# Gated recurrence in chunks of 64 tokens, two chunks side by side in the output partitions, in place of chunks of 128

## The chip, the cores and the metric

The kernel runs on one core of one Trainium2 chip. The time is device microseconds of one execution; the median of three runs is compared. The engines are TensorE (PE in the rows, with its weight loads as PEld), VectorE (DVE), ScalarE (ACT), GpSimd (POOL) and the DMA queues that SyncE (SP) and the others issue.

## What is computed

One inference step of one layer: a combined projection of 512 prompt tokens and 64 decode tokens (8 sequences of 8), a sparse attention with an indexer, a gated recurrence (HGRN2), an output projection and a layer norm. The change touches the recurrence alone. It has 4 heads with a 128x128 state each; the reference writes it chunk by chunk:

```python
cum = jnp.cumsum(gc, axis=2)
o_inter = jnp.einsum('bhtk,bhkv->bhtv', qc * jnp.exp(cum), S)
rel = jnp.where(causal, cum[:, :, :, None, :] - cum[:, :, None, :, :], -jnp.inf)
scores = jnp.einsum('bhtk,bhsk,bhtsk->bhts', qc, kc, jnp.exp(rel))
o_intra = jnp.einsum('bhts,bhsv->bhtv', scores, vc)
last = cum[:, :, -1:, :]
S_new = (jnp.exp(last[:, :, 0, :])[..., None] * S
         + jnp.einsum('bhsk,bhsv->bhkv', kc * jnp.exp(last - cum), vc))
```

The size of the chunk changes only the rounding of the result, not what is computed.

## The kernel before

**Layout.** Everything is float32. `qa`, `ky`, `cum`, `dec`, `kE` and `qE` lie with the 128 key dimensions in the partitions and 576 tokens (512 of the prompt, 64 of decode) by 4 heads in the free dimension. `ia` (the values), `sc` (the scores within a chunk) and `kdT` lie with tokens in the partitions.

**Scores within a chunk, by levels.** `exp(rel)` depends on both tokens and on the key dimension, so the kernel splits the causal triangle into levels. Level 0 is the diagonal. Level l > 0 has a block size b of 1, 2, 4, up to 64: a query in the right half of a block of 2b tokens meets a key in the left half, and both are scaled relative to the cumulative gate at the edge between the halves. For each level VectorE makes the right half of the differences into `dec` (L1389), GpSimd the left half (L1581), ScalarE takes the exponential of all of `dec` (L1114), GpSimd makes `kE` (L1591) and VectorE `qE` (L1460). TensorE multiplies `kE` by `qE` for a tile of 128 tokens and 4 heads: this is one job of a level (`level_job`, L808), and the levels with b below 8 have a fifth job for the decode tokens. VectorE copies the part that belongs to the level out of PSUM by a mask (`scores_out`, L1401) into `sc`.

**What they are interleaved with.** The same loops run the prompt attention: 32 pairs of a head and a block of 128 queries, pair a with block b = a % 4. A step is: logits (L821), masked row maximum on VectorE (L1409), exponential on ScalarE (L1092), transpose on TensorE (L830), copy of the transposed on ScalarE (`probs_out`, L1100), times values on TensorE (L839), scaled output on VectorE (L1421). The order is written out by hand: level l has three steps, from `LEAD + STEP * l` on, with `LEAD, STEP = 2, 3`. Three jobs stand in its first step and the others in its second. In the first step VectorE also makes the differences of level l + 1; ScalarE takes their exponential at the head of the second step, after `probs_out` of the first; VectorE makes `qE` in the third. The decay of the queries and of the keys to the end of the chunk follows at step `LAST`, `LAST + 1` and `LAST + 2`, where `LAST = LEAD + STEP * NLEV` is 26. The steps 29 to 31 and the two that drain have attention alone; the whole from step 26 on is called the tail here.

**The recurrence** stands in a second block, after all of this. TensorE turns `kE` into `kdT`, then for each of 4 chunks c makes the chunk's share of the state (L1694, into PSUM bank 4 + c % 2), turns a tile of the attention's output (`turn_gated`, L1680), and makes the output from the scores within the chunk (L1702) and from the state before it (L1706). VectorE makes the new state (`new_state`, L1899), copies the outputs (`outputs`, L1905) and then normalizes and gates (`norm_and_gate`, L1928). VectorE's order is `new_state(c)`, `outputs(c - 1)`, `mean_square(c - 2)`, `norm_and_gate(c - 3)`. GpSimd spreads decode values over `vx` (L1869), the last two when the outputs are done. TensorE goes on with `turn_normed(0)` (L1724), which waits for `norm_and_gate(0)`, then with the decode outputs (L1742, L1745) and the output projection (L1776) to the end.

## Time and profile before

| | |
|---|---|
| median of 3 runs | 785.72 us (784.81 to 791.41) |
| profiled execution, its own time | 787.79 us |
| its span, first to last instruction | 786.1 us |
| TensorE busy / weight loads | 734.3 us (93%) / 433.9 us |
| VectorE, ScalarE, GpSimd busy | 491.0, 265.0, 238.1 us |
| mean granted TensorE clock | 0.968 |
| levels with attention | 569 to 649 us |
| the tail | 649 to 676 us |
| recurrence, up to `turn_normed(0)` | 676 to 697 us |

A clock of 1.00 is 2.4 GHz and 0.50 is 1.2 GHz. A float32 matmul stands in the trace as two records of MATMUL and two of LDWEIGHTS, a transpose as one of each; so 12 matmuls are x24. Busy times are of one profiled execution.

### The profile page before, as it was taken

How to read it: one execution, taken by the hardware profiler on the slowest of the kernel's cores; microseconds unless marked ns; L12 is line 12 of the kernel's file. 1: busy time of each engine (PE TensorE's matmuls, PEld its weight loads, DVE VectorE, ACT ScalarE, POOL GpSimd, SP SyncE). 2: the span in 40 equal slices, each digit the busy share in tenths (PEclk: the TensorE clock that was granted, in tenths of full speed). 3: DMA queues.
4: the chain of work that ended last, by engine and by line, in shares of the span. 5: the costliest groups of instructions: out<-in, count | busy, mean ns of one | idle time of the engine just before them, and what ended most of it. 6: DMA issues, size and time to landing. Idle time of an engine off the chain costs nothing. (4 is left out here: it accounts for less than half of the span.)

```text
span 786.1 us, 13385 instructions
## 1 busy us (share of the span) xinstructions
PE 734.3 (93%) x4554; PEld 433.9 (55%) x4554; DVE 491.0 (62%) x923; ACT 265.0 (34%) x571; POOL 238.1 (30%) x342
## 2 busy tenths in 40 slices
PE   4688999999999899999999999999999997989994
PEld 3344444544444455767655566774477774864441
DVE  0213399999999546545555645555489985294535
ACT  3104710235665122223223222226556444340000
POOL 2610013046987223222222222221143461450000
PEclk9899999999999899999999999999999996699998
DMA  9900063060400588988888899861040000510611
GB/s 229 376 17 1 4 212 115 1 220 1 167 1 0 161 252 257 348 262 282 290 253 256 257 306 310 279 191 43 14 200 2 1 1 0 159 70 0 199 55 41
DMA packets 61316, 114.68 MB, mean 146 GB/s; under 512 B 8370, under 2 KB 21763, under 8 KB 61251
## 3 DMA queue, kind: packets, MB, share of 16 engines
q1 hardware_dynamic: 31122, 52.28, 21.7%
q0 software_dynamic: 12448, 40.27, 15.1%
q10 hardware_dynamic: 17680, 21.30, 8.1%
q8 instruction: 37, 0.61, 0.3%
q14 instruction: 29, 0.23, 0.1%
HBM read 106.60 MB, written 7.23 MB: 145 GB/s over the span
## 5 line engine op out<-in xcount | busy, mean ns | idle before, releaser
L473 PE MATMUL banks<-wbuf,xT 128*128 128x512 f32 (+1 forms) x448 | 147.4, 533 | 5.5 <-DMA wbuf<-in_w_in 5.5
L338 POOL DMA_DIRECT2D arena<-in_cache_v x128 | 70.0, 547 | 205.3 <-issue 205.3
L473 PEld LDWEIGHTS banks<-wbuf,xT 128*128 128x128 f32 (+1 forms) x448 | 65.8, 176 | 81.1 <-issue 70.8
L733 PE MATMUL banks<-wbuf,xT 128*128 128x512 f32 (+1 forms) x288 | 101.2, 531 | 0.0
L1262 DVE TENSOR_REDUCE small<-banks 128x1 f32<-128x512 f32 x32 | 22.1, 692 | 98.6 <-PE banks L664 98.6
L1220 DVE MAX8 small<-arena 64x8 f32<-64x2112 f32 x32 | 75.1, 2348 | 1.3
L1222 DVE MATCH_REPLACE8 arena<-small,arena 64x2112 f32<-64x2112 f32 x32 | 74.7, 2334 | 0.0
L647 PE MATMUL banks<-ident,arena 128*128 128x128 f32 x512 | 69.0, 278 | 4.1 <-DVE wbuf L1255 3.8
L647 PEld LDWEIGHTS banks<-ident,arena 128*128 128x128 f32 x512 | 57.1, 142 | 25.7 <-issue 19.3
L719 PE MATMUL banks<-xT,arena 128*128 128x288 f32 x256 | 67.4, 406 | 0.0
L1028 ACT COPY wbuf<-banks 128x512 f32<-128x512 f32 x64 | 37.2, 582 | 75.8 <-PE banks L647 69.8
L733 PEld LDWEIGHTS banks<-wbuf,xT 128*128 128x128 f32 (+1 forms) x288 | 41.0, 174 | 35.7 <-issue 32.8
L1035 ACT ACTIVATE arena<-banks,small 128x512 f32<-128x512 f32 x32 | 22.0, 688 | 96.5 <-DVE small L1262 96.5
L719 PEld LDWEIGHTS banks<-xT,arena 128*128 128x128 f32 x256 | 46.1, 190 | 10.1
L1503 POOL TENSOR_TENSOR arena<-arena,rope 128x64 f32<-128x64 f32 (+4 forms) x60 | 19.2, 350 | 93.8 <-ACT arena L890 92.4
L1537 POOL TENSOR_TENSOR late<-late,arena 128x256 f32<-128x256 f32 (+2 forms) x45 | 44.9, 999 | 6.0 <-ACT arena L964 0.8
L1255 DVE COPY wbuf<-banks 128x512 f32<-128x512 f32 x64 | 43.4, 679 | 0.8 <-PE banks L647 0.8
L808 PE MATMUL banks<-arena 128*128 128x128 f32 (+1 forms) x288 | 35.1, 275 | 6.1 <-DVE arena L1460 3.2
L808 PEld LDWEIGHTS banks<-arena 128*128 128x128 f32 (+1 forms) x288 | 31.9, 185 | 13.9 <-issue 9.7
L1275 DVE COPY arena<-banks 128x512 f32<-128x512 f32 x32 | 22.1, 689 | 27.3 <-PE banks L684 27.3
L695 PEld LDWEIGHTS banks<-arena 128*16 128x16 f32 x1024 | 25.1, 96 | 17.5 <-issue 17.5
L695 PE MATMUL banks<-arena 128*16 128x128 f32 x1024 | 34.1, 274 | 0.0
(256 smaller groups left out, 1139.7 us busy)
## 6 DMA issues: line engine op xcount, KB each, us to landing
arena<-in_cache_k SPq DMA_DIRECT2D x128, 256.0 KB, 3.4
arena<-in_cache_v POOLq DMA_DIRECT2D x128, 256.0 KB, 3.8
wbuf<-in_w_in ACTq DMA_DIRECT2D x8, 2048.0 KB, 12.8
arena<-in_w_in ACTq DMA_DIRECT2D x8, 512.0 KB, 6.0
arena<-in_x_prompt SPq DMA_DIRECT2D x8, 256.0 KB, 6.0
wbuf<-in_w_out SPq DMA_DIRECT2D x1, 2048.0 KB, 9.0
xT<-in_w_out SPq DMA_DIRECT2D x1, 2048.0 KB, 13.7
arena<-in_x_prompt SPq DMA_DIRECT2D x4, 512.0 KB, 8.4
```

The source lines that it names most:

```text
L338: e.dma_start(buf[n % 2][:, i, :], cache[bass.ds(pg, 1), 0].rearrange("a p h d -> p (a h d)")).then_inc(arrived[n % 2], 16)
L473: mm = pe.matmul(psum[a * NS:a * NS + ROWS[t], n % PB, 0:w // split], xT[:, c, t * P:t * P + ROWS[t]], wbuf[:, WB[g], c, a * w // split:(a ...
L647: mm = pe.transpose(psum[:, KB0 + j % 2, i * P:(i + 1) * P], k_buf[n % 2][:, i, j * P:(j + 1) * P], ident[:])
L695: mm = pe.matmul(psum[32 * j:32 * j + 16, OB, g * P:(g + 1) * P], pT[n % 2][:, i * P + 32 * j:i * P + 32 * j + 16], v_buf[n % 2][:, i, j * ...
L719: mm = pe.matmul(psum[:, FB, 0:HALF], w_f[m % 2][:, c, :], xT[:, c, half * HALF:(half + 1) * HALF], start=(c == 0), stop=(c == KC - 1), sk ...
L733: mm = pe.matmul(psum[a * NS:a * NS + ROWS[t], bank, 0:512 // split], xT[:, c, t * P:t * P + ROWS[t]], wbuf[:, WB[g], c, a * 512 // split: ...
L808: mm = pe.matmul(psum[0:w, n % 3, h * w:(h + 1) * w], kk[:, h, c0:c0 + w], qq[:, h, c0:c0 + w], start=True, stop=True, skip_group_check=True)
L1028: nc.scalar.copy(kg[n % 2][:, j, :], psum[:, KB0 + 1, :]).then_inc(kg_act, 1)
L1220: nc.vector.max(best[0:NS, 0, :], S).then_inc(topk, 1)
L1222: nc.vector.match_replace(S, best[0:NS, 0, :], S, TAKEN).then_inc(topk, 1)
L1255: nc.vector.tensor_copy(kg[n % 2][:, j, :], psum[:, KB0, :]).then_inc(kg_dve, 1)
L1537: nc.gpsimd.tensor_tensor(SP[b], SP[b], src, ALU.add).then_inc(pacc, 1)
```

## The change

A chunk is 64 tokens (`CH`), so the prompt has 8 chunks (`NC`) and the level with b = 64 is gone; `NLEV` is 7 and `LAST` is 23. Two chunks that follow each other still share a tile of 128 tokens: in a level job the first chunk's 64x64 scores go to partitions 0 to 63 and the second's to 64 to 127, by two matmuls for each head in place of one, and the mask and `sc` are half as wide. In the recurrence each step makes the shares of two states (keys and values from one half of the partitions each), the outputs within two chunks, then the outputs from the state before, for one chunk after the other, each in half of the output partitions. There are 8 state updates, and the outputs are copied from two banks, by halves of the partitions. The outputs of the second chunk now take banks 6 and 7 too, so `turn_normed(0)` and the decode outputs wait for the last of those copies (`oc_ev`). Two buffers that decode had shared with the masks have places of their own.

```diff
-LEVELS = [0, 1, 2, 4, 8, 16, 32, 64]
+LEVELS = [0, 1, 2, 4, 8, 16, 32]
+CH = 64
+NC = SEQ // CH
...
-        sc = carve(NT * 512).rearrange("p (c n) -> p c n", c=NT)
+        sc = carve(NT * HA * CH).rearrange("p (c n) -> p c n", c=NT)
...
-                    w, c0 = (P, c * P) if c < NT else (NS, SEQ)
                     for h in range(HA):
-                        mm = pe.matmul(psum[0:w, n % 3, h * w:(h + 1) * w], kk[:, h, c0:c0 + w], qq[:, h, c0:c0 + w],
-                                       start=True, stop=True, skip_group_check=True)
+                        for a in range(2 if c < NT else 1):
+                            c0 = c * P + a * CH
+                            mm = pe.matmul(psum[a * CH:(a + 1) * CH, n % 3, h * CH:(h + 1) * CH], kk[:, h, c0:c0 + CH],
+                                           qq[:, h, c0:c0 + CH], start=True, stop=True, skip_group_check=True)
                     mm.then_inc(lv, 1)
...
-                        out, mask, src = sc[:, c], levels[:, l], psum[:, n % 3, :]
+                        out, mask, src = sc[:, c], levels[:, l], psum[:, n % 3, 0:HA * CH]
...
-                for c in range(NT):
-                    pe.wait_ge(turned_ev, c + 1)
-                    if c >= 2:
-                        pe.wait_ge(st_ok, HA * (c - 1))
+                def chunk_states(t):
+
+                    pe.wait_ge(turned_ev, t + 1)
+                    if t:
+                        pe.wait_ge(st_ok, HA * 2 * t)
                     for h in range(HA):
-                        mm = pe.matmul(psum[:, 4 + c % 2, h * P:(h + 1) * P], kdT[:, c, h * P:(h + 1) * P],
-                                       ia[:, c, h * P:(h + 1) * P], start=True, stop=True, skip_group_check=True)
+                        for a in range(2):
+                            r = slice(a * CH, (a + 1) * CH)
+                            mm = pe.matmul(psum[:, 4 + a, h * P:(h + 1) * P], kdT[r, t, h * P:(h + 1) * P],
+                                           ia[r, t, h * P:(h + 1) * P], start=True, stop=True, skip_group_check=True)
                     mm.then_inc(kv, 1)
-                    turn_gated(c)
-                    if c >= 2:
-                        pe.wait_ge(oc_ev, c - 1)
+
+                def chunk_out(t, a):
+                    r = slice(a * CH, (a + 1) * CH)
+                    return r, psum[r, (2, 6)[a] + t % 2, :]
+
+                def within_chunks(t):
+                    if t >= 2:
+                        pe.wait_ge(oc_ev, t - 1)
                     for h in range(HA):
-                        out = psum[:, 2 + c % 2, h * P:(h + 1) * P]
-                        mm = pe.matmul(out, sc[:, c, h * P:(h + 1) * P], ia[:, c, h * P:(h + 1) * P],
-                                       start=True, stop=(c == 0), skip_group_check=True)
-                        if c:
-                            pe.wait_ge(st_ok, HA * c)
-                            mm = pe.matmul(out, qE[:, h, c * P:(c + 1) * P], states[(c - 1) % 2][:, h * P:(h + 1) * P],
-                                           start=False, stop=True, skip_group_check=True)
-                    mm.then_inc(oc, 1)
+                        for a in range(2):
+                            r, out = chunk_out(t, a)
+                            mm = pe.matmul(out[:, h * P:(h + 1) * P], sc[r, t, h * CH:(h + 1) * CH],
+                                           ia[r, t, h * P:(h + 1) * P], start=(h == 0), stop=(t == 0 and a == 0),
+                                           skip_group_check=True)
+
+                def from_before(t):
+                    for a in range(2):
+                        cc = 2 * t + a
+                        if cc == 0:
+                            continue
+                        pe.wait_ge(st_ok, HA * cc)
+                        r, out = chunk_out(t, a)
+                        for h in range(HA):
+                            mm = pe.matmul(out[:, h * P:(h + 1) * P], qE[:, h, cc * CH:(cc + 1) * CH],
+                                           states[(cc - 1) % 2][:, h * P:(h + 1) * P], start=False, stop=True,
+                                           skip_group_check=True)
+                        mm.then_inc(oc, 1)
+
+                for t in range(NT):
+                    chunk_states(t)
+                    turn_gated(t)
+                    within_chunks(t)
+                    from_before(t)
...
                     pe.wait_ge(mixed, t + 1)
+                    if t == 0:
+                        pe.wait_ge(oc_ev, NT)
...
                 values_apart(1)
-                pool.wait_ge(oc, NT)
+                pool.wait_ge(oc, NC - 1)
...
-                    dve.wait_ge(kv, c + 1)
+                    dve.wait_ge(kv, c // 2 + 1)
                     if c >= 2:
-                        dve.wait_ge(oc, c)
+                        dve.wait_ge(oc, c - 1)
...
-                        dve.wait_ge(oc, t + 1)
-                        nc.vector.tensor_copy(oa[:, t, :], psum[:, 2 + t % 2, :]).then_inc(oc_ev, 1)
+                        for a in range(2):
+                            r = slice(a * CH, (a + 1) * CH)
+                            dve.wait_ge(oc, 2 * t + a if t else 1)
+                            ins = nc.vector.tensor_copy(oa[r, t, :], psum[r, (2, 6)[a] + t % 2, :])
+                            if a == 0:
+                                me.add(ins)
+                        me.wait()
+                        ins.then_inc(oc_ev, 1)
...
                 for c in range(NT):
-                    new_state(c)
+                    new_state(2 * c)
+                    new_state(2 * c + 1)
                     if c >= 1:
                         outputs(c - 1)
```

TensorE in a middle level, before: logits (L821), three jobs (L808), a transpose and values of other steps (L830, L839), and in the second step the fourth job and the decode job.

```order
L821 MATMUL banks<-late 128x256
L808 MATMUL banks<-arena 128x128 x12
L830 MATMUL banks<-ident,wbuf 128x128
L839 MATMUL banks<-v_tok,wbuf 128x128 x4
L821 MATMUL banks<-late 128x384
L808 MATMUL banks<-arena 128x128 x4
L808 MATMUL banks<-arena 64x64 x4
L830 MATMUL banks<-ident,wbuf 128x128 x2
```

The same place after (line numbers are 4 higher):

```order
L825 MATMUL banks<-late 128x256
L812 MATMUL banks<-arena 64x64 x24
L834 MATMUL banks<-ident,wbuf 128x128
L843 MATMUL banks<-v_tok,wbuf 128x128 x4
L825 MATMUL banks<-late 128x384
L812 MATMUL banks<-arena 64x64 x12
L834 MATMUL banks<-ident,wbuf 128x128 x2
```

Nothing moved; 12 matmuls of 128 columns have become 24 of 64. The fourth job's 8 and the decode job's 4 are now one row of 12.

TensorE in the recurrence, the third chunk before: share of the state, `turn_gated`, and then for each head the two matmuls of the output.

```order
L1694 MATMUL banks<-arena 128x128 x4
L1680 MATMUL banks<-ident,late 128x128 x4
L1702 MATMUL banks<-arena 128x128
L1706 MATMUL banks<-arena 128x128
L1702 MATMUL banks<-arena 128x128
L1706 MATMUL banks<-arena 128x128
L1702 MATMUL banks<-arena 128x128
L1706 MATMUL banks<-arena 128x128
L1702 MATMUL banks<-arena 128x128
L1706 MATMUL banks<-arena 128x128
```

After, one pair of chunks (L1700 `chunk_states`, L1714 `within_chunks`, L1726 `from_before`):

```order
L1700 MATMUL banks<-arena 128x128 x8
L1683 MATMUL banks<-ident,late 128x128 x4
L1714 MATMUL banks<-arena 64x128 x8
L1726 MATMUL banks<-arena 64x128 x8
```

There are 24 matmuls where 12 stood, and all of those that read a state stand last.

VectorE at the end of the recurrence before: the last `new_state`, `outputs(2)`, `mean_square(1)`, `norm_and_gate(0)` (its reciprocal and four products), `outputs(3)`.

```order
L1899 SCALAR_TENSOR_TENSOR arena<-arena,banks 128x128 x4
L1905 COPY arena<-banks 128x512
L1919 TENSOR_SCALAR small<-small 128x4
L1925 RECIPROCAL small<-small 128x4
L1928 SCALAR_TENSOR_TENSOR arena<-arena,small 128x128 x4
L1905 COPY arena<-banks 128x512
```

The same place after:

```order
L1928 SCALAR_TENSOR_TENSOR arena<-arena,banks 128x128 x8
L1936 COPY arena<-banks 64x512 x2
L1954 TENSOR_SCALAR small<-small 128x4
L1960 RECIPROCAL small<-small 128x4
L1963 SCALAR_TENSOR_TENSOR arena<-arena,small 128x128 x4
L1936 COPY arena<-banks 64x512 x2
```

Two state updates and two half copies stand where one of each stood.

## Rows read from the trace of the kernel before

**Rows 1.** Stretches: us, busy us of PE, PEld, DVE, ACT, POOL, then PEclk, DMA.
```profile
615.00:625.00 10.00, 8.94 (x62) 7.05 (x61) 9.89 (x19) 4.92 (x10) 4.27 (x2) 1.00 0.01 2
...
652.00:654.50 2.50, 0.39 (x4) 0.18 (x3) 2.46 (x6) 0.04 (x1) 0.00 (x0) 0.92 0.00 0
...
661.00:676.20 15.20, 12.96 (x43) 8.98 (x42) 4.39 (x19) 3.48 (x10) 1.94 (x2) 0.50 0.00 1
676.20:681.40 5.20, 5.20 (x24) 4.51 (x25) 0.00 (x0) 2.90 (x5) 5.20 (x5) 0.50 0.67 189
...
692.60:697.00 4.40, 1.84 (x15) 1.25 (x14) 4.40 (x5) 1.37 (x10) 3.91 (x2) 1.00 0.20 60
697.00:701.90 4.90, 4.90 (x48) 3.90 (x50) 4.67 (x19) 2.06 (x11) 0.79 (x1) 0.65 0.02 3
```

**Rows 2.** Timeline of one middle level: start, us, engine, line.
```profile
621.73 2.75 PEld L808 LDWEIGHTS banks<-arena 128*128 128x128 f32 x24 [1.12 <-issue]
...
621.81 1.90 POOL L1581 TENSOR_TENSOR arena<-arena 128x1024 f32<-128x1024 f32 x1 [1.23 <-DVE arena L1460]
621.97 2.81 DVE L1389 TENSOR_TENSOR arena<-arena 128x1024 f32<-128x1024 f32 x1
...
625.05 1.95 DVE L1401 COPY_PREDICATED arena<-arena,banks 128x512 f32<-128x512 uint8 x3
...
625.67 0.24 ACT L1100 COPY wbuf<-banks 128x128 f32<-128x128 f32 x1
625.81 1.91 ACT L1114 ACTIVATE arena<-arena 128x2048 f32<-128x2048 f32 x1
...
627.80 2.35 POOL L1591 TENSOR_TENSOR arena<-arena 128x1024 f32<-128x1024 f32 x1 [4.10 <-ACT arena L1114]
...
629.76 1.47 DVE L1460 TENSOR_TENSOR arena<-arena 128x1024 f32<-128x1024 f32 x1
...
631.30 2.75 PEld L808 LDWEIGHTS banks<-arena 128*128 128x128 f32 x24 [1.05 <-issue]
```

**Rows 3.** Timeline: ahead of the exponential of the first level.
```profile
571.78 0.38 PE L830 MATMUL banks<-ident,wbuf 128*128 128x128 f32 x2
...
572.19 0.37 ACT L1100 COPY wbuf<-banks 128x256 f32<-128x256 f32 x1 [1.27 <-PE banks L830]
...
572.46 2.13 ACT L1114 ACTIVATE arena<-arena 128x2304 f32<-128x2304 f32 x1
```

**Rows 4.** Timeline: outputs of two attention steps in the tail.
```profile
664.33 0.28 DVE L1421 SCALAR_TENSOR_TENSOR late<-banks,small,late 128x64 f32<-128x64 f32 x1 [1.88 <-PE banks L839]
...
675.58 0.28 DVE L1421 SCALAR_TENSOR_TENSOR late<-banks,small,late 128x64 f32<-128x64 f32 x1 [2.23 <-PE banks L839]
```

**Rows 5.** Groups of one shape, 540 us to the end.
```profile
L1401 DVE COPY_PREDICATED arena<-arena,banks 64x256 f32<-64x256 uint8 x4 | 1.7, 425 | 0.0
...
L1990 DVE SCALAR_TENSOR_TENSOR arena<-arena,banks 64x512 f32<-64x512 f32 x1 | 0.7, 679 | 2.6 <-PE banks L1784 2.6
```

**Rows 6.** Timeline: weight loads of a 64-column job.
```profile
574.45 0.54 PEld L808 LDWEIGHTS banks<-arena 128*64 128x64 f32 x8
```

**Rows 7.** The chain that ended last: start, us, what.
```profile
686.49 0.89 PE banks L1694 x8
...
689.60 0.91 PE banks L1694 x8
...
690.53 1.12 DVE arena L1899 x4
...
692.45 4.43 DVE arena L1928 x4
...
696.92 0.66 PE banks L1724 x4
...
701.65 2.02 PE banks L1745 x32
```

**Rows 8.** Timeline of POOL in the recurrence.
```profile
692.80 3.91 POOL L1869 TENSOR_TENSOR arena<-arena,ofseq 64x1024 f32<-64x1024 f32 x2 [7.97 <-PE banks L1706]
```

More of the change, by code:

```diff
@@ L81, in shape_constants @@
     c["gather"] = np.concatenate([16 * (p // 16 == np.arange(8)[None, :]), p % 16], 1).astype(np.float32)
-    c["levels"] = lv.reshape(P, len(LEVELS) * P)
+    c["levels"] = lv.reshape(P, len(LEVELS) * CH)
     keep = np.ones((P, TOK), np.float32)
-    keep[:, 0:SEQ:P] = 0
+    keep[:, 0:SEQ:CH] = 0
     keep[:, SEQ::NNEW] = 0
@@ L351, in hybrid_step @@
         dec, cum, qE = (carve(4 * TOK).rearrange("p (h n) -> p h n", h=HA) for _ in range(3))
-        sc = carve(NT * 512).rearrange("p (c n) -> p c n", c=NT)
+        sc = carve(NT * HA * CH).rearrange("p (c n) -> p c n", c=NT)
         sc_n = carve(HA * NS)[0:NS]
-        levels_mem = carve(len(LEVELS) * HA * P // 4)
+        levels_mem = carve(len(LEVELS) * HA * CH // 4)
         levels = levels_mem.bitcast(U8).rearrange("p (l n) -> p l n", l=len(LEVELS))
-        levels_f = spare[:, 3072:3072 + len(LEVELS) * P].rearrange("p (l n) -> p l n", l=len(LEVELS))
+        levels_f = spare[:, 3072:3072 + len(LEVELS) * CH].rearrange("p (l n) -> p l n", l=len(LEVELS))
         states = [carve(HA * P) for _ in range(2)]
         seqcols = carve(NSEQ * NS)
+        apart_v, apart_q = carve(NSEQ * P), [carve(NSEQ * NS) for _ in range(2)]
         xflat = xT[:].rearrange("p c n -> p (c n)")
@@ L1370, in masks_in @@
                     for h in range(HA):
-                        me.add(nc.vector.tensor_copy(levels[:, :, h * P:(h + 1) * P], levels_f))
+                        me.add(nc.vector.tensor_copy(levels[:, :, h * CH:(h + 1) * CH], levels_f))
                     me.wait()
@@ L1436, in to_chunk_end @@
                     dve.wait_ge(qc_ok, 1)
-                    for (a, b, w) in ((0, SEQ, P), (SEQ, TOK, NNEW)):
+                    for (a, b, w) in ((0, SEQ, CH), (SEQ, TOK, NNEW)):
                         v = cum[:, :, a:b].rearrange("p h (n r) -> p h n r", r=w)
@@ L1619, in hybrid_step @@
         vx = [v[0:NS, a * 1024:(a + 1) * 1024].rearrange("p (s n) -> p s n", s=NSEQ)
-              for v in (vflat, scflat) for a in range(2)]
-        qx = [v.rearrange("p (s n) -> p s n", s=NSEQ) for v in (bias_p[:, 0:512], bias_p[:, 512:1024],
-                                                                levels_mem[:, 0:512], levels_mem[:, 512:1024])]
+              for v in (vflat, scflat, apart_v) for a in range(2) if a < v.shape[1] // 1024][0:HA]
+        qx = [v.rearrange("p (s n) -> p s n", s=NSEQ) for v in (bias_p[:, 0:512], bias_p[:, 512:1024], *apart_q)]
         sq = vflat[:, 2048:2048 + W2]
@@ L1653, in _ @@
                 sp.dma_start(lnb, ln_b.partition_broadcast(P)).then_inc(ln_in, 16)
-                sp.wait_ge(st_ok, HA * NT)
+                sp.wait_ge(st_ok, HA * NC)
                 sp.dma_start(st_prompt[0, 0].rearrange("h k v -> k h v"),
-                             states[(NT - 1) % 2].rearrange("p (h n) -> p h n", h=HA)).then_inc(state_st, 16)
+                             states[(NC - 1) % 2].rearrange("p (h n) -> p h n", h=HA)).then_inc(state_st, 16)
                 sp.wait_ge(skv_ev, HA)
@@ L1898, in new_state @@
                                 dve.wait_ge(st_ok, HA * c)
-                            nc.vector.scalar_tensor_tensor(st, old, el_p[:, h * NT + c:h * NT + c + 1], src,
+                            nc.vector.scalar_tensor_tensor(st, old, el_p[:, h * NC + c:h * NC + c + 1], src,
                                                            ALU.mult, ALU.add).then_inc(st_ok, 1)
```

13 lines of the change are left out of this document (7 added, 6 removed).

## The prediction

> **What bounds the kernel now.** I read the stretches first, then the timeline of one middle level, then the chain that ended last. The three places that the change touches have three different limits.
>
> In the levels (569 to 649 us) the limit is a ring through three engines, and the jobs of TensorE and the masked copies are not in it. Follow one level in [rows 2]. VectorE's `qE` product ends at 621.7 and TensorE's jobs begin. GpSimd makes its differences until 623.7, VectorE its own until 624.8. VectorE then has a row maximum, ScalarE an exponential of the attention and the copy `probs_out` at 625.67, and only then comes the exponential of the level, 625.81 to 627.72. GpSimd's product runs 627.80 to 630.15 and VectorE's `qE` product ends at 631.23, 1.1 us behind it. The next jobs begin at 631.30. The level took 9.57 us. The three jobs took 2.75 us and end at 624.5, ahead of the differences; the three masked copies took 1.95 us and end at 627.0, when VectorE's next product can't yet begin. The `qE` product shows the same: it was started at 629.76, ahead of the end of GpSimd's product, and still ended 1.1 us behind that end. So VectorE is busy nearly always here (9.89 of 10 us from 615 to 625, [rows 1]) and yet not the limit: what it gains in the copies it will spend waiting.
>
> In the tail TensorE runs at 1.2 GHz ([rows 1]: PEclk 0.50 from 661 on; it fell behind 652 to 654.5, where TensorE was busy 0.39 us of 2.50). It is busy 12.96 of 15.20 us, and four attention steps take 675.58 - 664.33 = 11.25 us [rows 4], 2.81 us each.
>
> In the recurrence the chain runs through TensorE and, at the end, VectorE [rows 7]: chunk 2 begins at 686.49, chunk 3 at 689.60, so 3.11 us a chunk; then the last state (1.12, from 690.53), a copy and two small operations (0.8 together), `norm_and_gate(0)` (4.43, from 692.45), and TensorE resumes at 696.92. From there TensorE is the limit to the end, so what resumes later ends later.
>
> **Prices of the new matmuls.** Eight records of 128 columns take 0.89 us (L1694, [rows 7]): 0.111 each. Eight weight loads of 64 columns with 64 moving columns take 0.54 us [rows 6], at most 0.068 a record. Do two halves of the output partitions run side by side? L1745 does what the change does: matmuls of 64 weight columns, alternating between the halves, 128 moving columns. Its 32 records took 2.02 us [rows 7], 0.063 each, where one after the other would need 0.111. They overlap. TensorE: Matmul & The Clock Gate, in the Trainium skill, says under Part 3 that weight loads overlap running matmuls only when the row groups differ. L1745's pairs share their row group, so this trace disagrees; by that rule the first and last level below would lose 1 us rather than gain 2.2, and the sum would be 3.2 us higher.
>
> A group of three jobs, 24 records and 2.75 us before, is 48 records: 48 x 0.068 / 2 = 1.6 us if the pairs overlap, 3.2 us if they do not. I take 1.6, since L1745 is the nearest row. In the middle levels either is hidden behind the differences (3.1 us after the jobs begin), so their jobs cost and save nothing. Without that cover, 3.2 us would cost 0.5 a level.
>
> **The masked copies.** A copy of 256 columns takes 0.425 us (64 partitions, [rows 5]) against 1.95 / 3 = 0.65: 28 copies save 6 us of VectorE. By the ring above I count zero; if VectorE were the limit it would be all 6.
>
> **The level that goes.** It takes 9.57 us with it. But the 32 attention steps stay, and three of them ran under it. They now run bare in the tail: 3 x 2.81 = 8.4. Gain 1.1 us. `LAST` comes three steps earlier and its work is the same. At 2.4 GHz the bare steps would be cheaper, so 8.4 is the upper end.
>
> **First and last level.** In the first the exponential (572.46) waited for `probs_out`, and that for the transposes at 571.78, which stand behind three jobs [rows 3]. With 1.6 for 2.75 all moves up 1.1 us. The last level has no differences under it, and its four jobs are in the path of the attention: 32 records at 0.111 are 3.6, 64 at 0.034 are 2.2. Of these 1.4 I take 1.1, since ScalarE has its own waits. Together -2.2, between +1 (no overlap) and -2.5.
>
> **The recurrence, ring.** Each pair of chunks now needs: shares of two states 16 x 0.063 = 1.0; `turn_gated` 4 x 0.111 = 0.44; within the chunks 16 x 0.063 = 1.0; the first chunk's output from its state 8 x 0.111 = 0.89. Only then may VectorE overwrite the older buffer with the second state (1.12), and the next pair's shares wait for that, since both their banks must be read. The second chunk's output (0.89) runs beside it. With 0.5 for draining, semaphores and changes of tile shape (my estimate, from the gaps of 0.02 to 0.1 us between engines in [rows 2]) it is 4.95 against 3.11. The first pair has no state to wait for at its start: +1.3. The next two: +1.84 each. So the fourth pair begins 5.0 us later.
>
> **The recurrence, end.** Before, from the start of chunk 3 to TensorE's resuming: 696.92 - 689.60 = 7.3. After, from the start of pair 3: 1.0 + 0.44 + 1.0 + 0.89 + 0.5 = 3.8; state 7, 1.12; `outputs(2)` is two copies, and a copy of 64 partitions costs the same as one of 128 (0.679 for 64x512, [rows 5]), so 1.3; two small operations 0.3 at most (0.8 less a copy). `norm_and_gate(0)` took 4.43 because it ran beside two GpSimd products of 3.91 us [rows 8]; those now begin about 1.7 us ahead of it, so it should end at about 9.2. TensorE must also wait for `outputs(3)`, 1.3 more, which stands behind it in VectorE's queue: before it was in nobody's way. That is 10.4, +3.1. Queued behind this new wait on TensorE are `turn_normed(0)`, the decode outputs and the projection. Both parts: +8.1 us.
>
> **The clock.** From 697 to 701.9 it was 0.65 [rows 1]: low for 3.4 us of 4.9, behind a wait of TensorE, which was busy 1.84 of the 4.40 us ahead of it. That wait grows from 2.5 to about 5 us, so I expect the low stretch to cover more of the decode outputs: +0.8, between 0 and 2. The head of the recurrence ran at 0.50 until 681.4 [rows 1]; the rise may come a little later with thinner work: +0.4, between 0 and 2.
>
> **Sum.** -1.1 - 2.2 + 5.0 + 3.1 + 1.2 = +6.0 us. The profiled execution took 787.79 us (span 786.1), so such a one would take 793.8; against the median of 785.72 it is **791.7 us**, 0.8% slower. About 1% (7.9 us) is what a measurement of this kernel can tell from no change.
>
> **Rivals.**
> - *The row halves do not run side by side (slower).* The shares of two states take their keys from partitions 0 to 63 and 64 to 127; no pair in this trace has different rows, so L1745 does not vouch for them. Then each of the eight groups costs 16 x 0.111 = 1.8, 0.8 more, all in the ring: +6.2, 798 us. It decides at a price of 0.078 a record, where the total passes 7.9. 15%.
> - *The clock (slower).* The levels keep TensorE less busy with jobs, and the recurrence has more waits. If it falls to 1.2 GHz in some levels, TensorE's work there becomes the limit for a while; if it does not rise in the recurrence, pieces of 3.3 us a pair double. 3 to 14 us more, 795 to 805; I put 798. For it: one short gap was enough at 652. Against: the levels had gaps of a microsecond ahead of each group of jobs [rows 2], and ran at 1.00 [rows 1]. 14%.
> - *VectorE is the limit in the levels after all.* -6 us: 786. Against it stands the `qE` product in [rows 2]. 9%.
> - *The clock stays up in the tail.* The gap at 652 falls otherwise, eight or more steps cost some 1.9 in place of 2.8 us (my estimate: TensorE's part halves, the other engines' part stays): -7, 785. 10%.
> - *The change does not do what it says:* the order shows the matmuls halved in width and doubled in number, and seven levels; under 1%.
>
> **How the numbers follow.** The forecast, 789 to 795, has 51%. A quarter of it lies past +1%; of the two slower rivals nearly all. The two that come out near the old time are within 1%, together a little below it in one case of four. So: slower 0.40, same 0.53, faster 0.07. The range has to hold both the clock's rivals and the row halves' price: 784 to 800 us.
>
> **What the profile after would show.** Middle levels still 9.6 us from jobs to jobs, VectorE with new idle time ahead of `qE`, masked copies near 0.4 us. Three jobs in about 1.6 us. Four bare steps in the tail still 11.2 us at 0.50. In the recurrence 4.9 us from pair to pair, `turn_normed(0)` released by `outputs(3)` some 29 us after the block's start in place of 20.7. I am wrong if the levels shrink with the copies, if the pairs of 16 records take 1.8 us, or if the clock behaves otherwise.

## The result and the profile after

The changed kernel takes 789.88 us (median of 20 runs, 786.34 to 794.28) beside 787.08 us for the kernel before (20 runs). The ratio is 1.0037, with a 95% interval of 1.0019 to 1.0054: 2.9 us slower, within the 1% that the prediction called no change. The profiled execution took 789.72 us, its span is 788.1 (before 786.1), its mean clock 0.960 (before 0.968).

Line numbers after: jobs L812, masked copies L1405, exponential of a level L1118, differences L1585 (GpSimd) and L1393 (VectorE), `kE` L1595, `qE` L1464, `new_state` L1928, `outputs` L1936, `mean_square` L1954, `norm_and_gate` L1963, `turn_normed` L1753.

**Stretches after**, which answer to [rows 1]: us, busy us of PE, PEld, DVE, ACT, POOL, then PEclk, DMA.

```profile
...
605.00:615.00 10.00, 8.21 (x94) 5.53 (x93) 9.06 (x17) 4.39 (x11) 4.23 (x2) 1.00 0.01 2
651.00:666.00 15.00, 15.00 (x49) 10.21 (x49) 4.54 (x21) 5.15 (x15) 0.00 (x0) 0.50 0.01 2
669.70:673.00 3.30, 2.79 (x22) 2.09 (x22) 0.00 (x0) 2.15 (x4) 3.24 (x3) 1.00 0.43 98
693.40:697.90 4.50, 1.12 (x4) 0.72 (x4) 4.37 (x9) 1.69 (x10) 1.70 (x1) 0.57 0.09 28
697.90:705.90 8.00, 7.93 (x76) 6.48 (x76) 5.13 (x21) 2.06 (x11) 2.52 (x2) 0.60 0.00 0
...
```

In the levels VectorE is busy 9.06 of 10 us where it was 9.89. The tail is at 0.50, as before. But the head of the recurrence (669.7 to 673) is at 1.00, where it was at 0.50. Ahead of `turn_normed(0)` TensorE is busy 1.12 of 4.50 us, and the decode outputs behind it have a mean clock of 0.60.

**One middle level after**, and the jobs of the two that follow, as [rows 2]: start, us, engine, line.

```profile
...
609.65 1.51 PEld L812 LDWEIGHTS banks<-arena 128*64 128x64 f32 x48 [1.27 <-issue]
...
609.72 1.90 POOL L1585 TENSOR_TENSOR arena<-arena 128x1024 f32<-128x1024 f32 x1 [1.22 <-DVE arena L1464]
609.89 2.81 DVE L1393 TENSOR_TENSOR arena<-arena 128x1024 f32<-128x1024 f32 x1
...
613.10 1.10 DVE L1405 COPY_PREDICATED arena<-arena,banks 128x256 f32<-128x256 uint8 x3
...
614.08 1.91 ACT L1118 ACTIVATE arena<-arena 128x2048 f32<-128x2048 f32 x1
...
616.06 3.45 POOL L1595 TENSOR_TENSOR arena<-arena 128x1024 f32<-128x1024 f32 x1 [4.44 <-ACT arena L1118]
...
616.06 1.22 DVE L1464 TENSOR_TENSOR arena<-arena 128x1024 f32<-128x1024 f32 x1
...
619.54 1.23 DVE L1393 TENSOR_TENSOR arena<-arena 128x1024 f32<-128x1024 f32 x1 [1.08 <-POOL arena L1595]
619.59 2.93 POOL L1585 TENSOR_TENSOR arena<-arena 128x1024 f32<-128x1024 f32 x1
619.62 1.51 PEld L812 LDWEIGHTS banks<-arena 128*64 128x64 f32 x48 [1.33 <-issue]
...
622.61 1.91 ACT L1118 ACTIVATE arena<-arena 128x2048 f32<-128x2048 f32 x1 [0.72 <-POOL arena L1585]
...
628.11 1.51 PEld L812 LDWEIGHTS banks<-arena 128*64 128x64 f32 x48 [1.44 <-issue]
...
```

The three jobs take 1.51 us (before 2.75, and by [rows 6] at most 3.2) and the three masked copies 1.10 (1.95), and the level still takes 619.62 - 609.65 = 9.97 us (9.93 before at this place). What VectorE saved in the copies went into idle time, and into waiting inside a `qE` product that starts earlier: the one ahead of this level takes 2.99 us, before 2.48. At 616.06 something is new: the exponential has ended and VectorE is free, so its `qE` product and GpSimd's `kE` product start together. VectorE's takes 1.22 us and GpSimd's 3.45, which ends at 619.51. At the differences of the next level VectorE is first again (1.23, GpSimd 2.93 beside it). That level takes 628.11 - 619.62 = 8.49 us, where the one before took 9.57. All of the gain lies ahead of its exponential, which starts 2.99 us behind the jobs (622.61); in [rows 2] it is 4.08. From the exponential to the next jobs both take 5.5 us.

**The first level after**, as [rows 3], and **two attention outputs in the tail**, as [rows 4]:

```profile
...
568.49 1.48 PEld L812 LDWEIGHTS banks<-arena 128*64 128x64 f32 x48 [0.55 <-issue]
...
570.03 0.20 PEld L834 LDWEIGHTS banks<-ident,wbuf 128*128 128x128 f32 x2
...
570.78 2.13 ACT L1118 ACTIVATE arena<-arena 128x2304 f32<-128x2304 f32 x1
...
```

```profile
...
653.05 0.28 DVE L1425 SCALAR_TENSOR_TENSOR late<-banks,small,late 128x64 f32<-128x64 f32 x1 [0.98 <-PE banks L843]
...
665.66 0.28 DVE L1425 SCALAR_TENSOR_TENSOR late<-banks,small,late 128x64 f32<-128x64 f32 x1 [0.98 <-PE banks L843]
...
```

The transposes start 1.5 us behind the jobs and the exponential at 570.78; the first level takes 577.43 - 568.49 = 8.94 us, before 10.13. Four steps of attention in the tail take 12.6 us (667.50 - 656.10 = 11.4 for others), where [rows 4] had 11.25.

**The masked copy after**, as [rows 5]: busy us, mean ns.

```profile
...
L1405 DVE COPY_PREDICATED arena<-arena,banks 128x256 f32<-128x256 uint8 x28 | 11.1, 439 | 0.7 <-PE banks L812 0.6
...
```

**The chain after**, through the recurrence, as [rows 7]:

```profile
...
673.04 1.09 PE banks L1700 x16
...
674.72 1.02 PE banks L1714 x16
675.74 1.02 PE banks L1726 x8
676.76 1.09 PE banks L1700 x16
...
681.84 1.16 PE banks L1700 x16
...
686.99 1.16 PE banks L1700 x16
...
691.14 0.86 DVE arena L1928 x3
692.00 0.59 DVE arena L1936
...
693.35 1.78 DVE small L1954
...
695.51 0.87 DVE arena L1963 x3
...
697.13 0.70 DVE arena L1936
...
697.97 1.08 PE banks L1753 x4
...
```

The four pairs of chunks begin at 673.04, 676.76, 681.84 and 686.99: 3.7, 5.1 and 5.15 us each. Sixteen records take 1.09 us for the shares of two states and 1.02 within the chunks. Read the end from 686.99: the last state from 690.9, two half copies from 692.00, then `mean_square` with 1.78 us for four numbers a partition, `norm_and_gate`, and the second half copy of `outputs(3)`, which releases TensorE at 697.97. GpSimd's pass over the values, as [rows 8], lies over it:

```profile
...
691.36 3.74 POOL L1898 TENSOR_TENSOR arena<-arena,ofseq 64x1024 f32<-64x1024 f32 x2 [12.95 <-PE banks L1726]
...
```

The traces of all kernels, one execution each, cut at three places that each has. The first column of times goes from the first level's jobs to the first transpose of the recurrence's block, the second to `turn_normed(0)`, the third to the output projection, the fourth to the end. The sum leaves out what lies ahead of the levels, which the edits hardly touch and which differs by up to 4 us between executions. The ratio is that of the timed runs, of which each experiment has 6 to 12, to the median of the kernel before in the same session (787.35 to 787.88 us). It says what a change is worth; the profile says where, within the scatter of a single execution.

| kernel | levels, tail | recurrence | to projection | rest | sum | low clock in the tail | ratio, 95% |
|---|---|---|---|---|---|---|---|
| before | 107.2 | 20.7 | 7.1 | 82.1 | 217.1 | 27.3 us | 1 |
| after | 101.3 | 28.2 | 8.4 | 81.8 | 219.6 | 27.3 | 1.0037, 1.0019 to 1.0054 |
| e1 seven levels | 105.5 | 19.1 | 5.5 | 81.8 | 211.8 | 27.3 | 0.9898, 0.985 to 0.9946 |
| e2 half copies | 107.2 | 20.5 | 7.1 | 82.1 | 217.0 | 27.3 | 0.9993, 0.9963 to 1.0024 |
| e3 old recurrence | 103.0 | 19.1 | 8.2 | 81.8 | 212.0 | 27.3 | 0.9875, 0.9827 to 0.9923 |
| e4 eighth level | 102.0 | 28.2 | 8.5 | 81.8 | 220.4 | 17.1 | 1.0041, 1.0012 to 1.007 |
| e5 values held, before | 107.2 | 18.0 | 10.6 | 83.8 | 219.6 | 27.3 | 1.0042, 1.0019 to 1.0064 |
| e6 values held, after | 101.9 | 26.6 | 7.9 | 81.8 | 218.2 | 27.3 | 1.0011, 0.9989 to 1.0032 |
| e9 three edits, after | 102.0 | 24.7 | 7.1 | 81.8 | 215.6 | 27.3 | 0.9995, 0.9978 to 1.0013 |
| e10 narrow jobs, before | 104.2 | 19.1 | 5.5 | 82.1 | 210.9 | 17.1 | 0.9966, 0.9947 to 0.9986 |
| e12 products held, before | 107.2 | 20.7 | 7.1 | 82.1 | 217.1 | 27.3 | 0.9984, 0.996 to 1.0009 |
| e13 both held, before | 108.8 | 18.2 | 5.7 | 82.1 | 214.9 | 27.3 | 0.9951, 0.9926 to 0.9977 |
| e14 = e10 and e13 | 104.6 | 18.1 | 5.7 | 82.1 | 210.6 | 27.3 | 0.9909, 0.9876 to 0.9942 |
| e15 = e9, products held | 101.8 | 24.8 | 7.1 | 81.8 | 215.4 | 27.3 | 0.9986, 0.9956 to 1.0015 |

So the changed kernel gained 5.9 us in levels and tail, and lost 7.5 in the recurrence and 1.3 behind it.

### The profile page after: what moved, and what is told of

It reads as the page before. It is cut to its first block and busy times, and to the rows that moved or that the text cites. A ratio compares the mean times of both kernels' runs of the same rounds, so it can differ in the third digit from the quotient of the medians.

```text
span 788.1 us, 13973 instructions
## 1 busy us (share of the span) xinstructions
PE 730.1 (93%) x4842; PEld 423.4 (54%) x4842; DVE 478.3 (61%) x937; ACT 263.0 (33%) x570; POOL 235.0 (30%) x340
## 5 line engine op out<-in xcount | busy, mean ns | idle before, releaser
L736 PEld LDWEIGHTS banks<-wbuf,xT 128*128 128x128 f32 (+1 forms) x288 | 40.4, 172 | 35.2 <-issue 32.2
L1279 DVE COPY arena<-banks 128x512 f32<-128x512 f32 x32 | 22.0, 689 | 27.3 <-PE banks L687 27.3
L667 PE MATMUL banks<-wbuf,arena 128*32 128x512 f32 x256 | 34.1, 605 | 0.0
L1096 ACT ACTIVATE wbuf<-wbuf,small 128x128 f32<-128x128 f32 (+3 forms) x32 | 17.9, 559 | 44.2 <-DVE small L1413 44.1
```

The lines of the kernel that those rows point to most:

```text
L736: mm = pe.matmul(psum[a * NS:a * NS + ROWS[t], bank, 0:512 // split], xT[:, c, t * P:t * P + ROWS[t]], wbuf[:, WB[g], c, a * 512 // split: ...
```

## The experiments

### Which half of the change does what

**e1: before, without the level b = 64** (the scores between the two halves of a chunk are missing; all else as before).

```diff
-LEVELS = [0, 1, 2, 4, 8, 16, 32, 64]
+LEVELS = [0, 1, 2, 4, 8, 16, 32]
...
```

> The kernel before with the level of b = 64 left out and nothing else changed: chunks, jobs, copies and recurrence stay 128 tokens wide, so the scores between the two halves of each chunk are missing from the output. It prices the level alone. Theory R (the levels are a ring through VectorE, ScalarE and GpSimd, and the attention steps that ran under the level run bare in the tail afterwards): 9.6 us go, three bare steps of 2.8 us come at 1.2 GHz, so 1 to 2 us faster. Rival V (the level was a cost of its own, and attention is hidden anyway): 6 to 9 us faster.

Levels and tail became 1.7 us shorter, not 9.6: three attention steps that ran under the level now run bare. The rest of the 5.3 us that the profile shows from the first level on (1.7 us up to `turn_normed(0)`, 1.6 behind it) is clock: its low stretch ended 2.9 us ahead of the recurrence, where the one of before ended 5.2 us inside it, and it did not fall a second time. The timed runs miss the expectation: six of them are 8.0 us faster than before (4.2 to 11.8), more than the 1 to 2 us of theory R and in the range of rival V. In the profiled execution 2.1 us of it lie ahead of the levels. So the timed runs of e1 do not decide between the two; the 1.7 us in its profile and e4 do.

**e2: before, with masked copies of half the width** (256 of the 512 columns of each job are copied, the other scores are missing).

```diff
-                        out, mask, src = sc[:, c], levels[:, l], psum[:, n % 3, :]
+                        out, mask, src = sc[:, c, 0:256], levels[:, l, 0:256], psum[:, n % 3, 0:256]
```

> The kernel before, with eight levels, where each masked copy takes 256 of the 512 columns; the other half of the scores is missing from the output. Each of the 32 copies of the prompt falls from 0.65 to about 0.37 us. Theory R: the copies are outside the ring, so 0 to 2 us faster, the 2 by a changed order of VectorE and GpSimd at the products. Rival V (VectorE, busy 9.9 of 10 us there, is the limit): 32 x 0.28, about 8 us faster.

One level of it, timeline:

```profile
...
623.84 1.10 DVE L1401 COPY_PREDICATED arena<-arena,banks 128x256 f32<-128x256 uint8 x3
...
626.59 2.35 POOL L1591 TENSOR_TENSOR arena<-arena 128x1024 f32<-128x1024 f32 x1 [4.10 <-ACT arena L1114]
...
628.55 1.47 DVE L1460 TENSOR_TENSOR arena<-arena 128x1024 f32<-128x1024 f32 x1
...
630.09 1.08 PEld L808 LDWEIGHTS banks<-arena 128*128 128x128 f32 x9 [1.05 <-issue]
...
```

The three copies take 1.10 us in place of 1.95. GpSimd's product ends at 628.94 and VectorE's still at 630.02, 1.1 us behind it; the level takes 630.09 - 620.53 = 9.56 us, before 9.57. Levels and tail: 107.2 and 107.2. The copies are in nobody's way, and the rival with VectorE as the limit falls.

**e3: the changed levels with the recurrence of before** (the scores of two chunks are read as if they were one of 128 tokens, so the outputs of the recurrence are others; the work has the size of before).

```diff
...
+                        mm = pe.matmul(out, sc[:, c, (h % 2) * P:(h % 2 + 1) * P], ia[:, c, h * P:(h + 1) * P],
+                                       start=True, stop=(c == 0), skip_group_check=True)
...
```

> The changed kernel's seven levels with 64-token jobs, but the recurrence of the kernel before: 4 steps of 128 tokens, 4 state updates, one output copy a step, none of the new waits. Scores are read from a buffer of another layout, so prompt outputs and states of the recurrence are not the reference's. It prices the recurrence. Theory R, with the two traces: the recurrence costs 7.5 us and the lower clock behind it 1.3, so this is 6 us (0.7%) faster than the kernel before, and 8 to 9 faster than the changed one. Rival (the loss is in the levels, or is noise of the clock): within 2 us of the changed kernel.

The recurrence takes 19.1 us and not 28.2, with the same clock of 1.00 at its head. So the eight updates, with their copies and waits, cost 9.1 us in the profile; between the ratios of e3 and of the changed kernel it is 1.6%, 12.8 us, with an uncertainty of about 4. And against the kernel before it gains 4.2 us in levels and tail and 1.7 at the head of the recurrence, where only the clock differs. Its timed runs are 9.8 us faster than before (6.1 to 13.6), where 6 had been expected.

**e4: the changed kernel with an eighth level** (its mask is zero everywhere, so it adds nothing to the scores).

```diff
-LEVELS = [0, 1, 2, 4, 8, 16, 32]
+LEVELS = [0, 1, 2, 4, 8, 16, 32, 64]
```

> The changed kernel with an eighth level again: b = 64, with masks that are zero in every 64-token chunk, so that its jobs, differences, exponential, products and masked copies run and change nothing in the output. Theory R: 9.6 us of a level come, three bare steps of 2.8 us go, so 1 to 2.5 us slower than the changed kernel, 4 to 6 slower than the kernel before. Rival V: 8 us or more slower than the changed kernel, 11 or more than the kernel before.

Levels and tail: 102.0 us, where the other kernels with the changed levels took 101.3 to 103.0. In the timed runs it cannot be told from the changed kernel: 1.0041 and 1.0037, so 0.3 us apart, between -2.4 and +3.0. That holds the 1 to 2.5 us of theory R, and the 8 us of rival V fall. The level of 9.65 us (629.20 to 638.85) is nearly free, because it carries three attention steps. In its profile the low stretch of the tail was 17.1 us in place of 27.3, so that the small price in the table is a lower bound.

**e10: before, with the jobs in 64x64 blocks**, eight levels, copies 512 wide. The level 64 is one block for each head.

```diff
...
+                    elif LEVELS[l] == NS:
+                        blocks = [(0, NS, P, c * P, c * P + NS)]
+                    else:
+                        blocks = [(a * NS, a * NS, P, c * P + a * NS, c * P + a * NS) for a in range(2)]
...
```

> The kernel before, chunks of 128 tokens and all eight levels, but the score jobs of a level issued as the changed kernel issues them: 64x64 blocks, the two halves of the block in the two halves of the output partitions; level 64 then is one block per head. The copies out of PSUM stay 512 wide. It tells the rewritten jobs from the dropped level. Theory (the jobs' shape matters only where TensorE is the limit, at the first and the last level, 1.1 us each): 785.5, 2 to 3 us below before. Rival (no level is bound by TensorE, the first and last gains of the changed kernel come of the copies): 788, ratio 0.999 to 1.001.

2.7 us faster (0.9966). In its profile the first level takes 8.96 us (before 10.13), and from the last level's jobs to the recurrence it is 32.6 (before 35.2), 1.1 of it because the low stretch was 17.1 us; in e14, where it was 27.3, this part is 33.7. So the narrower block of the jobs, which needs no chunk of 64, gives 1.2 us at the first level and 1.5 at the last. The 8.49 us level is not there: neither half-wide copies (9.56) nor narrow jobs (9.56) alone make it, and all six kernels that have both have it (8.48 to 8.50). For the narrow jobs alone this is less sure: in e10 a fall of the clock lay over the levels just ahead (between 605.5 and 616.5 us), and in e14 one lay over the start of this level itself. Why VectorE comes free early enough only with both I did not take apart.

### What the recurrence waits for

**e5: before, GpSimd's pass over the values held** until the first norm and gate is done.

```diff
                 pool.wait_ge(oc, NT)
+                pool.wait_ge(mixed, 1)
                 values_apart(2)
```

> The kernel before, and GpSimd alone waits for VectorE's mixed operand before it starts its 3.9 us pass over the next pair's values (L1869 there), so that the pass no longer shares time with VectorE's norm and gate of token tile 0. Theory (VectorE's two short instructions were stretched by GpSimd's pass): norm and gate takes 1.1 us instead of 4.43, TensorE resumes some 2.2 us earlier, and with 1 us less of it at the low clock behind: 785 us beside a before of 788, 2 to 3.5 us below it. Rival (GpSimd's pass is needed by then, its values come late for chunk pair 2): what VectorE gains, the scores of the next pair lose; 788 to 790.

A miss: 1.0042, slower than before. The recurrence became 2.7 us shorter, as expected, and the next stretch 3.5 longer. VectorE, then GpSimd, then TensorE:

```profile
...
693.41 1.14 DVE L1929 SCALAR_TENSOR_TENSOR arena<-arena,small 128x128 f32<-128x128 f32 x4
...
696.74 7.57 DVE L1929 SCALAR_TENSOR_TENSOR arena<-arena,small 128x128 f32<-128x128 f32 x4
...
694.71 3.75 POOL L1869 TENSOR_TENSOR arena<-arena,ofseq 64x1024 f32<-64x1024 f32 x2 [8.69 <-DVE arena L1929]
698.44 7.63 POOL L1881 TENSOR_TENSOR wbuf<-wbuf,arena 128x1024 f32<-128x1024 f32 x4
...
698.64 1.97 PE L1745 MATMUL banks<-wbuf,arena 128*64 128x128 f32 x32
705.62 0.74 PE L1724 MATMUL banks<-ident,arena 128*128 128x128 f32 x4 [5.01 <-DVE late L1951]
...
```

The first norm and gate takes 1.14 us and not 4.43. But the four products over the decode states (L1881), which GpSimd now starts at 698.44, meet the second one: 7.57 us in place of 1.14. TensorE has its decode outputs done at 700.6 and waits until 705.62 for it. The clock's 3.4 us low stretch, which before lies ahead of the projection, now lies at its start (between 705.5 and 709.5), and the last column of the table is 1.7 us longer. The contention was moved to a worse place, and neither of my two theories had named it.

**e12: before, the products alone held**, until the fourth norm and gate; **e13: both held.** The second hold is

```diff
+                pool.wait_ge(mixed, NT)
                 for h in range(HA):
 
                     pool.wait_ge(dec_o, h // 2 + 1)
```

> The kernel before, and GpSimd alone waits for the fourth norm and gate before it starts its four products over the decode states (L1880 there, 7.75 us, which ran beside the fourth norm and gate and stretched it to 7.49). Nobody waits for that norm for 10 us more, and the products are first needed at 719.9, so both theories expect no change: 787 to 788, ratio 0.998 to 1.002. It is the control of the two runs beside it.

> The kernel before with both GpSimd passes held: the one over the values until the first norm and gate is done, the four products until the fourth is. Theory (holding the first pass gained 2.7 us up to the resuming of TensorE and lost it because the products then ran beside the second norm and gate, 7.57 us, for which TensorE waited 5.0): the gain stays, 2.5 to 4 us below the kernel before, ratio 0.995 to 0.997. Rival (the passes can't be moved without a price, since the decode outputs wait for the values): level with the kernel before or above, ratio 1.000 to 1.004.

e12 is level with before (0.9984, interval with 1 in it), and its profile has the same stages to 0.02 us. e13 is 3.9 us faster (0.9951): recurrence 18.2 us, next stretch 5.7. Its trace, in the order VectorE, GpSimd, TensorE:

```profile
...
694.36 1.14 DVE L1930 SCALAR_TENSOR_TENSOR arena<-arena,small 128x128 f32<-128x128 f32 x4
...
696.02 1.55 DVE L1921 TENSOR_SCALAR small<-small 128x4 f32<-128x4 f32 x1
...
697.68 2.65 DVE L1930 SCALAR_TENSOR_TENSOR arena<-arena,small 128x128 f32<-128x128 f32 x4
...
695.65 3.74 POOL L1869 TENSOR_TENSOR arena<-arena,ofseq 64x1024 f32<-64x1024 f32 x2 [8.90 <-DVE arena L1930]
704.29 7.50 POOL L1882 TENSOR_TENSOR wbuf<-wbuf,arena 128x1024 f32<-128x1024 f32 x4 [4.90 <-DVE arena L1930]
...
696.43 0.60 PE L1724 MATMUL banks<-ident,arena 128*128 128x128 f32 x4
...
701.65 0.63 PE L1724 MATMUL banks<-ident,arena 128*128 128x128 f32 x4
...
```

The first norm and gate takes 1.14 us. GpSimd's pass (695.65 to 699.39) now lies over the second mean square (1.55 us, ending at 697.57 with GpSimd's first instruction) and the second norm (2.65), for neither of which TensorE waits: the second transposes come at 701.65, behind the decode outputs. The products start at 704.29, and only the last norm, of decode, is beside them. The hold gained nothing by itself and 3.9 us with the other.

**e6: the changed kernel, values held.** The edit is that of e5.

> The changed kernel with the same wait of GpSimd. Theory: the mean square of token tile 0, 1.78 us beside GpSimd's pass in the changed kernel's profile, takes about 0.1 and norm and gate stays at 1.1, so TensorE resumes 1.7 to 2 us earlier: 2 to 3 us below the changed kernel, level with the one before (0.997 to 1.001). Rival (the stretch is of VectorE's own making): no difference from the changed kernel, ratio 1.003 to 1.004.

The recurrence takes 26.6 us and not 28.2. `mean_square` went from 1.78 to 0.17 us:

```profile
...
694.91 0.17 DVE L1955 TENSOR_SCALAR small<-small 128x4 f32<-128x4 f32 x1
...
```

1.0011 and 1.0037: 2 us, as expected, but the two intervals overlap and the rival's 1.003 lies inside this one. What decides is the profile, not the timed runs.

**e9: the changed kernel with three edits:** values held, `turn_normed(0)` into bank 2 so that it need not wait for `outputs(3)`, and `turn_gated` ahead of `chunk_states`.

```diff
...
                 for t in range(NT):
-                    chunk_states(t)
                     turn_gated(t)
+                    chunk_states(t)
...
                     if t == 0:
-                        pe.wait_ge(oc_ev, NT)
+                        pe.wait_ge(oc_ev, NT - 1)
...
```

> The changed kernel with three edits of its recurrence: GpSimd's pass held back as in the run beside it (-1.9 us), the transposes of the gated tile 0 put into another PSUM bank so that they don't wait for the last evacuation of the outputs (-1.4), and the transposes of a chunk pair's gated tile issued ahead of its chunk states, in the 1.1 us in which TensorE waits anyway (-1.8 = 3 x 0.59). Theory: the recurrence's price is these waits, and they can be filled: 5 us below the changed kernel, some 2 below the one before, ratio 0.996 to 0.999. Rival (the chain through the state update is the limit wherever the other work stands): only the first two count, and the ratio stays at 1.000 to 1.001.

TensorE in its recurrence:

```profile
...
685.01 1.16 PE L1700 MATMUL banks<-arena 64*128 64x128 f32 x16 [0.28 <-DVE arena L1929]
...
689.71 1.16 PE L1700 MATMUL banks<-arena 64*128 64x128 f32 x16 [0.28 <-DVE arena L1929]
...
697.29 0.66 PE L1741 MATMUL banks<-ident,arena 128*128 128x128 f32 x4 [2.40 <-ACT late L1838]
697.79 1.00 PE L1753 MATMUL banks<-ident,arena 128*128 128x128 f32 x4
...
```

The pairs come 4.56 and 4.70 us apart in place of 5.15, the wait ahead of a pair is 0.28 in place of 0.87. So 0.59 and 0.45 us are gained. `turn_normed(0)` comes at 697.79 behind other transposes (L1741, of the attention's outputs for the decode tokens), which waited 2.40 us for a ScalarE copy (L1838); ScalarE had the four squares of tile 2 ahead of it. From the last pair to `turn_normed(0)` it is 8.1 us, in e6 9.4; 0.6 of that is the transposes which now stand ahead of the pair, so the other bank gave 0.7 of its 1.4 us. Recurrence: 24.7 us. The ratio of 0.9995 lies between what the two theories gave, and its interval holds both.

**e14: before with narrow jobs and both holds; e15: e9 with both holds.**

> The kernel before with the narrow jobs and both holds, chunks of 128 tokens and all eight levels. If the two gains stand in different places they add: -2.7 (narrow jobs, ratio 0.9966) and -2.5 to -4: 781 to 783, ratio 0.991 to 0.994. Rival (only the one or the other counts, the end follows the projection's loads): 784, 0.996 to 0.998.

> The changed kernel with its recurrence mended in three places as before and the four products held too. In the run without the second hold TensorE went from the first turned tile to the projection in 7.1 us, at the low clock for half of it and with no wait for VectorE, so I expect nothing from the second hold: 786 to 787, ratio 0.998 to 1.000. If the products cost something there that the profile does not show, 785 or less. Beside the run with narrow jobs and both holds it compares the best form of either size of chunk: the chunks of 128 should be some 4 us ahead.

e14 takes 779.64 us, 0.9909 (0.9876 to 0.9942): 7 us faster than before, where 5 to 7 had been expected: the two gains (2.7 and 3.9) add. e15 stays at 0.9986 as expected. So the best form with chunks of 128 is 0.8%, 6 us, ahead of the best with chunks of 64, give or take 3.5. e14 beats both kernels.

## Why the prediction was right, and where its sum was off

The direction, the range and the kind of outcome were right. The forecast was +6.0 us; the profile has +1.9 and the timed runs +2.9, half of it. Term by term, forecast and measured in the profiles:

| term | forecast | measured |
|---|---|---|
| first level | -1.1 | -1.2 |
| middle levels | 0 | -1.5 |
| level removed, and last level | -2.2 | -3.2 |
| clock at the head of the recurrence | +0.4 | -1.3 |
| recurrence, ring | +5.0 | +5.2 |
| recurrence, end | +3.1 | +3.6 |
| clock behind it | +0.8 | +1.3 |
| ahead of the levels, and the projection | 0 | -0.9 |

The measured terms add up to +2.0. The terms of the levels and of the head's clock came out 4.3 us below the forecast, those of the recurrence and the clock behind it 1.2 above, and 0.9 lies outside the change, within what executions differ by. So it was the recurrence, forecast at +8.1 and measured at +8.8, that kept the direction right. That the forecast time of 791.7 us lies only 1.8 above the measured 789.88 is partly luck: it was built on the median of three runs, 785.72, where twenty gave 787.08.

*Right and shown.* The ring through ScalarE and the two products sets the levels, not VectorE's copies (e2). A level is worth far less than its 9.6 us, because its attention steps stay: in e1's profile 1.7 in levels and tail, 3.4 with the head of the recurrence, which the low clock left; e4's timed runs exclude 8 us, those of e1 don't. Rewritten jobs count at the first and last level (e10, e14), and by 0.2 us at one more (e14: 10.73 for 10.95). Pairs of halves overlap in the array: three jobs 1.51 us (forecast 1.6), two state shares 1.09 (1.0); the rival with 1.8 us falls. The recurrence pays 9 us for eight updates (e3), 5.2 of it in the ring (forecast 4.95 a pair, measured 5.1), and `outputs(3)` is what releases TensorE.

*The step that was mis-sized most in the levels is their zero.* "Their jobs cost and save nothing" held for three of five middle levels. One took 10.54 us for 10.95 (10.71 to 10.75 in e4, e6, e9 and e15), the other 8.49 for 9.57. In the level ahead of the latter the order of the two products turned over, and so VectorE came first at the differences too, which took 1.1 us off. The signs of it stood in [rows 2]: the second of the two products waits for the first, so which is first matters, and VectorE's idle time decides it. I had counted that idle time as worth nothing.

*The clock at the head had the wrong sign.* I expected thinner work to delay the rise. But the low stretch has lasted 27.3 us in twelve of the fourteen profiles and began with the idle gap of TensorE at the start of the tail; with more bare steps behind that gap, it ended 3 us ahead of the recurrence (666.7) and not 5.2 inside it. The rival with a fall inside the levels half came true: all eight kernels with narrow jobs have one at about 590 us, and of the six with wide jobs only e13. In the level ahead of it TensorE was busy 7.81 of 10.77 us after, 9.44 of 11.10 before. The fall (588.2, for 3.4 us) cost nothing, since the narrow jobs had room (2.67 us; level 10.62, before 10.63); in e13, with the wide jobs of before (4.38 us), one at the same place made the level 12.1 us.

*The last level and the one removed.* e1 has -1.7 for the removal (forecast -1.1); the rest is 1.5 in this profile and 1.0 to 1.2 in e6, e9 and e15. In e1 the three bare steps took 9.6 - 1.7 = 7.9 us, 2.6 each, where I had 2.8 as the upper end; single groups of four took 11.4 and 12.6 us at 0.50 in the changed kernel, not a steady 11.2.

*The end* came to 11.0 us where I had 10.4. Its parts were not those that I named: I had put what is left of GpSimd's pass on `norm_and_gate`, and it fell on `mean_square` (1.78 us; 0.17 in e6). The wait for `outputs(3)` was 1.4, forecast 1.3.

## What to carry to other kernels

Ask of a stage that is to be removed what runs under it: here 9.6 us of level were worth 1.7 us of levels and tail (e1), since the work beneath it stays. A serial chain that is cut in more pieces pays its waits for each piece, and the halved instructions don't give it back: a pair of chunks of 64 took 5.15 us for the 3.11 of one chunk of 128, and a copy of 64 partitions 0.70 for 0.68. Where two engines exclude each other, moving one of them moves the stretched instruction, so look at what it will meet there before it is moved; e5 lost 3.3 us by a wait that gained 3.9 once the next collision was moved too.

## What the runs showed of the hardware

**VectorE and GpSimd take turns.** While GpSimd was in a product, a VectorE instruction with two operands in SBUF waited for its end: four products of `norm_and_gate` beside four GpSimd products of 1.9 us took 7.57 us (e5), alone 1.14. A small `mean_square` of 128x4 took 1.55 and 1.78 us in place of 0.17, though it has one operand. A copy out of PSUM was not stretched: 0.69 us in e5 (L1906 there, at 694.47, beside GpSimd's pass from 694.71), 0.68 without GpSimd. And it goes the other way: with VectorE first, `qE` took 1.22 us and GpSimd's product 3.45 instead of 2.35. The Trainium skill (SBUF — State Buffer, Who interferes with whom) says that the pair of ports that the two share is an exclusive lock, which VectorE takes with two SBUF inputs or in a 2-port mode, `tensor_scalar` among them, and that who starts first decides who blocks. These traces agree: the products of `norm_and_gate` and of `qE` have both operands in SBUF, `mean_square` is a `tensor_scalar`, the copy reads PSUM, and `qE` held GpSimd up where it was first.

**Halves of the array.** Sixteen records with operands in different row halves took 1.09 us (L1700), sixteen with both rows and columns apart 1.02 (L1714), 0.064 to 0.068 each, and 48 with one row group and different column halves 1.51 (0.031 each, with 64 columns). Eight that kept to one half (L1726) took 1.02, 0.128 each. By the rule of the Trainium skill that the prediction quotes (TensorE: Matmul & The Clock Gate, Part 3), that weight loads overlap only where row groups differ, the 48 would not have overlapped. They did, in every kernel with narrow jobs: 0.031 a record, where those that stay in one half take 0.068 [rows 6].

**The clock's low stretches.** In the tail the clock fell to 0.50 for 27.3 us in twelve profiles and for 17.1 in two (e4, e10). Behind the recurrence it fell for 3.4 us before, for 10.2 in the changed kernel, for 6.8 and 3.4 in e6 and e9 with their shorter waits ahead of it, and not at all in e1, e10, e13 and e14. The fall of 3.4 us is worth 1.6 us: 7.1 against 5.5 us to the projection. What starts a fall is not settled by these runs: e13 and the kernel before have the same instructions up to 590 us, and only e13 fell there.
